# Prompt attention of a two-layer trunk: from head pairs in a loop to single heads in a pipeline, and PSUM banks released one by one

## What is computed

```python
def latent_attention(q_lat, q_pe, rows, q_pos, k_pos):
    c_kv, k_pe = rows[:, :KV_LORA], rows[:, KV_LORA:]
    s = (jnp.einsum('qhr,kr->hqk', q_lat, c_kv, preferred_element_type=jnp.float32)
         + jnp.einsum('qhp,kp->hqk', q_pe, k_pe, preferred_element_type=jnp.float32)) * SOFTMAX_SCALE
    s = jnp.where(k_pos[None, None, :] <= q_pos[None, :, None], s, NEG_INF)
    p = jax.nn.softmax(s, axis=-1)
...
        hp = layer_norm(ALPHA * hp + mix_p, ln_g[i, 0], ln_b[i, 0])
        hp = layer_norm(ALPHA * hp + swiglu(hp, ffn_w_gate[i], ffn_w_up[i], ffn_w_down[i]), ln_g[i, 1], ln_b[i, 1])
```

## Time and profile before

| | us |
|---|---|
| median of three executions | 2686.84 (2685.57 to 2687.7) |
| the profiled execution, its own time | 2684.7 |
| span of its instructions | 2682.9 |
| PE busy with matmuls | 2553.1 (95% of the span) |
| DVE / ACT / POOL busy | 1005.3 / 567.6 / 585.6 |
| mean granted TensorE clock | 0.974 of full speed |

### The profile page before, as it was taken

The page is one execution under the profiler, slowest core; times in us unless marked ns, Lnnn a source line. Parts: engine busy times, 40 slices in busy tenths (PEclk is TensorE's granted clock), DMA queues, the critical chain, the costliest instruction groups (busy, mean ns, idle before and its releaser), DMA issues.

```text
span 2682.9 us, 34788 instructions
## 1 busy us (share of the span) xinstructions
PE 2553.1 (95%) x13203; PEld 2122.1 (79%) x13203; DVE 1005.3 (37%) x1489; ACT 567.6 (21%) x948; POOL 585.6 (22%) x290
## 2 busy tenths in 40 slices
PE   8899999999999889899999999988999999999996
PEld 7789888898889776585857584447889988899885
DVE  3433333333333642333333333422333333333336
ACT  2411011110111342332323232433111111111112
POOL 2422222222222410000000000232222222222225
PEclk9999999999999989999999999988999999999998
DMA  5201110111101111000000002232101111011111
GB/s 165 55 24 47 47 47 23 47 47 47 47 23 47 44 48 43 16 1 31 0 19 12 16 0 75 80 122 55 46 25 47 47 47 40 30 47 47 47 31 67
DMA packets 130114, 117.37 MB, mean 44 GB/s; under 512 B 8704, under 2 KB 117208, under 8 KB 130048
## 3 DMA queue, kind: packets, MB, share of 16 engines
q1 hardware_dynamic: 130064, 116.70, 14.6%
HBM read 110.81 MB, written 6.42 MB: 44 GB/s over the span
## 4 chain that ended last, share of the span: by engine, by line
PE 92%; DVE 4%; issue 2%; ACT 1%; POOL 0%; DMA 0%; SPq 0%; ACTq 0%; DVEq 0%
PE ps L557 22%; PE ps L558 21%; PE ps L559 21%; PE ps L922 4%; PE ps L911 4%; PE ps L806 2%; PE ps L895 2%; PE ps L978 1%; PE ps L780 1%; PE ps L822 1%; PE ps L811 1%; PE ps L627 1%; PE ps L953 1%; PE ps L851 1%; PE ps L937 1%
## 5 line engine op out<-in xcount | busy, mean ns | idle before, releaser
L557 PE MATMUL ps<-XH,WGH 128*128 128x368 f32 x2112 | 699.8, 331 | 17.6 <-POOL WGL L1700 13.5
L558 PE MATMUL ps<-XL,WGH 128*128 128x368 f32 x2112 | 700.0, 331 | 0.0
L559 PE MATMUL ps<-XH,WGL 128*128 128x368 f32 x2112 | 697.2, 330 | 0.0
L1452 DVE TENSOR_TENSOR XR<-XR,ps 128x1024 f32<-128x1024 f32 x378 | 461.5, 1221 | 105.7 <-PE ps L559 105.7
L557 PEld LDWEIGHTS ps<-XH,WGH 128*128 128x128 f32 x2112 | 398.5, 189 | 22.3 <-issue 18.9
L1437 DVE TENSOR_TENSOR HF<-SG,ps 128x368 f32<-128x368 f32 x132 | 71.0, 538 | 917.8 <-PE ps L559 912.6
L558 PEld LDWEIGHTS ps<-XL,WGH 128*128 128x128 f32 x2112 | 398.0, 188 | 1.8
L559 PEld LDWEIGHTS ps<-XH,WGL 128*128 128x128 f32 x2112 | 398.2, 189 | 0.0
L557 PE MATMUL ps<-WDH,HH 128*128 128x512 f32 (+1 forms) x792 | 329.4, 416 | 9.6 <-DVE XR L1452 9.6
L1691 POOL TENSOR_TENSOR HL<-HF,HH 128x368 fp32r<-128x368 f32 x132 | 129.8, 983 | 853.0 <-DVE HH L1441 853.0
L559 PE MATMUL ps<-WDH,HL 128*128 128x512 f32 (+1 forms) x792 | 314.9, 398 | 0.0
(11 more groups left out here) (205 smaller groups left out, 2725.8 us busy)
## 6 DMA issues: line engine op xcount, KB each, us to landing
RAWG<-ffn_w_gate SPq DMA_DIRECT2D x44, 512.0 KB, 4.7
RAWG<-ffn_w_up SPq DMA_DIRECT2D x44, 512.0 KB, 5.9
RAWD<-ffn_w_down SPq DMA_DIRECT2D x44, 512.0 KB, 3.7
CR<-cache_mla_l SPq DMA_DIRECT2D x64, 160.0 KB, 2.6
XR<-x_prompt SPq DMA_DIRECT2D x8, 512.0 KB, 12.4
WOP<-mla_w_o SPq DMA_DIRECT2D x4, 1024.0 KB, 5.0
WOA<-mla_w_o SPq DMA_DIRECT2D x1, 4096.0 KB, 17.3
o_y_prompt<-XR SPq DMA_DIRECT2D x8, 512.0 KB, 2.6
```

The source lines that it names most:

```text
L557: pe.matmul(out, w[0], x[0], start=start, stop=False)
L558: pe.matmul(out, w[0], x[1], start=False, stop=False)
L559: return pe.matmul(out, w[1], x[0], start=False, stop=stop)
L1452: dve.tensor_tensor(XR[0:r, t, :], XR[0:r, t, :], bank2(4 + 2 * w, r), ALU.add).then_inc(s_row[2 * l + 1], 1)
```

## The change

- **Attention.** The loop of head pairs becomes one straight list of 72 units, head by head. Between the steps of a unit PE issues "side" pieces from a list (`SIDE`, `PLAN`): the 11 projection pieces of the next head and the 16 output pieces (one matmul of 512 columns each) of the head before, up to three pieces in a unit: one ahead of the transposes, one ahead of the value product, one behind it. Head 0's projections come before all units, the last head's output pieces after them. `SHARE` says how many pieces each unit takes.
- **Banks.** Scores of even units use banks 0 and 1, those of odd units bank 2; a piece that doesn't fit goes to bank 6 (`EXTRA`). Value products and output transposes use bank 3, probability transposes 4 and 5, side pieces 6 and 7 in turn, but 7 alone while bank 6 is held for scores.
- **Values** are projected for one head at a time (128 columns for each weight load instead of 256). An output piece is added to `XR` by DVE on its own (512 columns).
- **Meta unit.** Its scores have 80 rows instead of 16, and transposes and value products always take 128 rows. POOL clears the columns of `PR` behind a unit's keys.
- **SwiGLU.** `down_tile`, `last_down` and `down_add` wait, signal and add by banks of 512 columns instead of pairs.
- The weights of a head are loaded on their own, two heads ahead. `c_band_meta` has 80 rows.

```diff
+BANKS = 4
+SHARE = ([(1, 1, 0)] * 5 + [(0, 1, 0)] + [(0, 0, 0)] * 3, [(1, 1, 1)] * 9, [(0, 0, 0)] + [(0, 1, 1)] * 8)
...
+        EXTRA = 6
+        ORDER = ((7, 8, 6, 0, 5, 1, 4, 2, 3), (0, 7, 8, 6, 3, 5, 1, 4, 2))
+        UNITS = [(h, q) for h in range(H) for q in ORDER[h % 2]]
...
+                for x_, n_ in enumerate(parts):
+                    PLAN[-1].append(range(len(SIDE), len(SIDE) + n_))
+                    SIDE += own[:n_]
+                    own = own[n_:]
+                    later = range(u_, u_ + 2) if x_ == 0 else range(u_ + 1, u_ + 3)
+                    held = any(extra(e) for e in later if e < NU)
+                    for f_ in range(n_):
+                        BANK.append(13 - EXTRA if held else 13 - BANK[-1] if BANK[-1] in (6, 7) else 6)
...
 # PE, down_tile
-                pe.wait_ge(s_row[2 * l + 1], NT * n + t + 1)
                 for half in (0, 1):
                     ds = slice(half * 512, half * 512 + 512)
-                    ins = split_product(ps[0:r, 4 + 2 * w + half, :], (HH[:, b, cols(t)], HL[:, b, cols(t)]),
-                                        (WDH[:, ds], WDL[:, ds]), True, True)
-                ins.then_inc(f_dmm[l], 1)
+                    pe.wait_ge(s_row[2 * l + 1], 2 * NT * n + 2 * t + half + 1)
+                    split_product(ps[0:r, 4 + 2 * w + half, :], (HH[:, b, cols(t)], HL[:, b, cols(t)]),
+                                  (WDH[:, ds], WDL[:, ds]), True, True).then_inc(f_dmm[l], 1)
...
 # PE, attention
+            def side(f):
+                kind, h, k = SIDE[f]
+                s, b = h % 2, BANK[f]
+                before = [x for x in range(f) if BANK[x] == b]
+                if before:
+                    wait_side(pe, before[-1])
...
+            for u in range(NU):
+                groups = chunks(UNITS[u][1])
+                for f in PLAN[u][0]:
+                    side(f)
+                pe.wait_ge(h_ex, ex_count(u))
+                pe.wait_ge(h_z, u + 1)
+                for x, g in enumerate(groups):
+                    if x == 2:
+                        followers(u)
+                    probability_group(u, x, g)
+                if len(groups) < 3:
+                    followers(u)
+                for f in PLAN[u][1]:
+                    side(f)
+                values(u)
+                for f in PLAN[u][2]:
+                    side(f)
...
 # ACT, attention
+            for u in range(NU):
+                h = UNITS[u][0]
+                for f in PLAN[u][0]:
+                    side_act(f)
+                if u >= 1:
+                    output_rows(u - 1)
+                if u + 1 < NU:
+                    exponentials(u + 1)
+                for x, g in enumerate(chunks(UNITS[u][1])):
+                    k = GROUP_AT[u] + x
+                    if k % 2 == 0:
+                        evacuate_probabilities(act, copy, u, k, g).then_inc(h_ta, 1)
+                for part in PLAN[u][1:]:
+                    for f in part:
+                        side_act(f)
+                if u % NQ == 2 and h + 1 < H:
+                    rope_queries(h + 1)
...
 # DVE, down_add
-                dve.tensor_tensor(XR[0:r, t, :], XR[0:r, t, :], bank2(4 + 2 * w, r), ALU.add
-                                  ).then_inc(s_row[2 * l + 1], 1)
+                for half in (0, 1):
+                    ds = slice(half * 512, half * 512 + 512)
+                    dve.wait_ge(f_dmm[l], 1 + 2 * NT * n + 2 * t + half + 1)
+                    dve.wait_ge(s_row[2 * l + 1], 2 * NT * n + 2 * t + half + 1)
+                    dve.tensor_tensor(XR[0:r, t, ds], XR[0:r, t, ds], ps[0:r, 4 + 2 * w + half, :], ALU.add
+                                      ).then_inc(s_row[2 * l + 1], 1)
...
 # POOL, attention
+            for u in range(NU):
+                n = unit_q(UNITS[u][1])[2]
+                if u >= 2:
+                    pool.wait_ge(h_t, GROUP_AT[u - 1])
+                pool.memset(PR[:, u % 2, n:(n + P - 1) // P * P], 0.0).then_inc(h_z, 1)
```

More of the change, by code:

```diff
@@ L290, in pieces @@
[L290 to L315, removed]
+        KSPLIT = (0, 352, 704, KEYS)
+        def projection(h):
+            return ([("q", h, k) for k in range(3)] + [("k", h, k) for k in range(3)] + [("t", h, 0)]
+                    + [("v", h, k) for k in range(3)] + [("l", h, 0)])
+        def output(h):
+            return [("o", h, k) for k in range(2 * (NT - 1))]
@@ new lines, in hybrid_trunk @@
+        SIDE = projection(0)
+        BANK = [f % 4 for f in range(len(SIDE))]
+        PLAN = []
+        for h_ in range(H):
+            own = (projection(h_ + 1) if h_ + 1 < H else []) + (output(h_ - 1) if h_ > 0 else [])
+            share = SHARE[0 if h_ == 0 else 2 if h_ == H - 1 else 1]
+            assert sum(sum(x) for x in share) == len(own) and len(share) == NQ
+            for parts in share:
+                PLAN.append([])
+                u_ = len(PLAN) - 1
+                for x_, n_ in enumerate(parts):
[6 more added lines that the diff above has]
+                        BANK.append(13 - EXTRA if held else 13 - BANK[-1] if BANK[-1] in (6, 7) else 6)
@@ new lines, in wait_side, with wait_projection, evacuate_side @@
+        def wait_side(eng, f):
+            if f in SIDE_DVE:
+                eng.wait_ge(h_fd, dve_sides(f))
+            else:
+                eng.wait_ge(h_fa, act_sides(f))
+        def wait_projection(eng, h):
+            last = SIDE.index(("l", h, 0))
+            eng.wait_ge(h_fa, act_sides(last))
+            eng.wait_ge(h_fd, dve_sides(last))
+        def evacuate_side(eng, copy, f, low):
+            kind, h, k = SIDE[f]
+            s = h % 2
+            b = BANK[f]
+            src = ps[:, b, :]
+            eng.wait_ge(h_fill, f + 1)
@@ new lines, in scores @@
+            def scores(u):
+                h, q = UNITS[u]
+                if u % NQ == 0:
+                    wait_projection(pe, h)
+                    pe.wait_ge(h_ql, h + 1)
+                if extra(u) and u >= 2:
+                    before = [f for f in range(PLAN[u - 2][1].start) if BANK[f] == EXTRA]
+                    if before:
+                        wait_side(pe, before[-1])
+                for bank, lo, hi in pieces(u):
+                    ins = score_piece(u, bank, lo, hi)
+                ins.then_inc(h_s, 1)
@@ new lines, in values @@
+            def values(u):
+                h, q = UNITS[u]
+                ta, td = groups_done(u)
+                pe.wait_ge(h_ta, ta)
+                if td:
+                    pe.wait_ge(h_td, td)
+                if u >= 1:
+                    pe.wait_ge(h_te, u)
+                last = (unit_q(q)[2] - 1) // P
+                for c in range(last + 1):
+                    ins = pe.matmul(ps[:, 3, 0:VH], PTS[:, u % 2, c, :], VT[:, c, h % 2, :],
+                                    start=(c == 0), stop=(c == last))
+                ins.then_inc(h_pv, 1)
@@ new lines, in _ @@
+            for f in range(len(projection(0))):
+                side(f)
+            pe.wait_ge(h_kr, 2)
+            pe.wait_ge(h_init, 3)
+            scores(0)
+            scores(1)
+            for u in range(NU):
[6 more added lines that the diff above has]
+                    if x == 2:
+                        followers(u)
+                    probability_group(u, x, g)
[5 more added lines that the diff above has]
+                for f in PLAN[u][2]:
+                    side(f)
@@ L929, in page_unit @@
+            out_transpose(NU - 1)
+            for f in LAST_SIDE:
+                side(f)
+            pe.wait_ge(h_fa, len(SIDE_ACT))
+            pe.wait_ge(h_fd, len(SIDE_DVE))
             def page_unit(s, k, b):
```

585 lines of the change are left out of this document (287 added, 298 removed).

## The result

| | before | after | ratio, 95% interval |
|---|---|---|---|
| first comparison, median of 4 runs each | 2686.20 us | 2614.94 us | 0.9742 (0.9720 to 0.9764) |
| the changed kernel again, in a later comparison (7 and 4 runs) | 2683.88 us | 2624.12 us | 0.9776 (0.9760 to 0.9792) |

Forecast: 2651 us, range 2612 to 2679. The change gained 71 us in the first comparison and 60 in the second, where 36 were forecast. So the question is where 24 to 35 us came from that no term of the sum held.

The account below looks back on a forecast made before the run. PE, busy 95% of the span, was taken as the bound. Terms -30 + 2 - 62 + 4 + 50 = -36 against 2684.7 us gave 2649, or 2651 us at the median; range 2612 to 2679 us.

Parts of the forecast that it names:

- Banks in the down pass: SwiGLU down passes: PE's wait for DVE's add goes when banks are freed singly, 40 x 0.75 = -30 us.
- Last down passes: Down passes at each layer's end, where DVE is the bound: two adds replace one, +2 us (0 to +4).
- Stalls that go: Prompt attention: all present PE stalls vanish except the very first queries' 1.8 us, -62 us.
- Change no number of columns that matter; nothing, between -1 and +1: Attention: more rows in meta scores, transposes and value products cost PE nothing, between -1 and +1 us.
- +4 us to the value pieces: Attention value projections by single heads: 36 matmuls of 128 columns at 0.246 us, 8.86 for 7.88 us, four times.
- New waits: Attention pipeline: PE waits for ORW (16 + 15 us), shared banks (18) and list ends (1), sum +50 us.
- full cover: Rival: the attention pipeline covers nearly all, new waits 10 to 25 us instead of 50; 2619 us, chance 0.27.
- Clock, slower than before: Rival: many 1 to 2 us waits in each attention head keep lowering the clock; 2695 us, chance 0.08.
- DVE bounds the pass: Rival: half adds cost DVE 0.72 us or more, so down passes gain only -10; 2671 us, chance 0.10.
- The attention gives nothing at all: Rival: attention waits of 58 us and more, only down passes gain; 2659 us, within the forecast's own range.
- What was to show it: Profile signs: 12.5 us down passes without the wait, attention about 545 us, ORW and bank 7 waits, projection-only stage only for head 0.

Follow-up runs that it names:

- experiment 2: Changed kernel with the meta band (its load and matmuls) cut back to 16 rows: 2631.45 us, ratio 0.9779.
- experiment 6: Kernel before with down passes by single banks, the 80-row band and last value chunks on 128 partitions, but no pipeline: 2617.53 us, ratio 0.9756.
- experiment 1: Kernel before with only the down-pass edits of the change (banks given back singly, adds of 512 columns): 2648.95 us, ratio 0.9859.
- experiments 7 to 9: Changed kernel with ORW copied at its own step's end (2606.90 us), then also rotary work on POOL (2593.73 us), then also side pieces redistributed (2586.89 us).

## Why the forecast was right in sign and 24 to 35 us short

1. *Banks in the down pass, -30*: right. 40 x (13.24 - 12.50) = -30 us, and the two stages together gave -31 to -33. DVE's adds take 0.69 us and are no bound, so that rival fell.
2. *Last down passes, +2*: not seen; nothing in the stages of the SwiGLUs is left for it (-31 to -33 in all, where -28 was forecast).
3. *Stalls that go, -62*: a little too large. Before, PE idled 553.2 - 518.1 = 35 us in the attention and spent 34 us at half clock, worth 17 at most: 52 us. After: 45 us idle, 7 to 14 us at half clock, 48 to 52 us. Both sums leave out some 8 us, by my estimate: the views show such a matmul 0.275 us long where they start 0.112 apart, so idle time is some 0.16 us short at each wait, of which there are 48 before and 52 after. With it the stalls before come to 60 us, and the new waits to 53.
4. ***"Change no number of columns that matter; nothing, between -1 and +1"*: this is the step that failed.** The 80-row band is worth -7 to -8 us (experiment 2) and the full last chunk -24 to -27 us (experiment 6); of the product I had counted columns only, of the band I had written nothing, and left out that a matmul on 16 rows costs more than one on 128 when its neighbours have 128. The row I had in hand says it: the eight value products of the earlier trace rows end with the short one, and 1.97 us over eight gave me "0.246 each", where seven stand at 0.224 and the last takes the rest, 0.40. With that mean I then charged +4 us to the value pieces; they take 36 x 0.111 = 4.0 us a head, 8.0 for a pair against 7.88, so +0.5 for the four pairs.
5. *New waits, +50*: right as a sum (44.9 us of idle time) and in kind, in part by luck in the sizes. For `ORW` PE waited 19.6 us (forecast 16 + 15): 12.6 behind the rotary copies, 2.7 us three times, 1.0 three times and 1.4 once (forecast 2.3 seven times), and 7 behind projection pieces. At shared banks and low parts it was 16 us (forecast 18). Another 9 us of waits of other kinds, for `VT`, `PR`, `QPS` and `OT` above all, stood in no line of the forecast and made up most of the difference.

So in the attention the pipeline's old stalls and new waits cancel, and experiment 6 shows just that: +2 to +5 us. Add -24 in the value products, -8 at the start, -31 to -33 in the SwiGLU stages and -2 in the latents (most of it there with the edit of experiment 1 alone, its cause not tried): -60 to -65 us, against -60.6 between the profile of before and that of the later comparison. In the first comparison the sample attention, at a higher clock, adds 8 to 9.

The result lies in the stated range by luck: the range was drawn down to 2612 us to take in full cover, and full cover did not happen.

*The rivals.* "Full cover" had said 2619 us, the number nearest to the result, and its mechanism did not happen: PE still waited 45 us. It came only with experiments 7 to 9, and then the kernel stood at 2587. "Clock, slower than before" fell: the clock in the attention went up (0.97 to 0.99) with 10 us more of idle time. "DVE bounds the pass" fell with 12.47 us. "The attention gives nothing at all" is what the pipeline did, but not the whole change.

*What was to show it.* Right: the pass of 12.5 us, the adds of 0.69, the wait of the weight load gone, `ORW` behind the rotary copies once a head (though 1.0 to 2.7 us), the waits at shared banks. Wrong: the attention at 545 us; it took 531 to 534.

Still open: why the clock in the sample attention takes one of two courses with the same work, between comparisons and within one.

## What to carry to other kernels

Count changes of tile size as well as columns: a matmul on 16 or 64 partitions between matmuls on 128 cost 0.34 to 0.38 us here for the round trip, the same for either, so pad it with zeros if it stands alone and put short ones side by side if there are more. When a rewrite wins, run the old structure with the rewrite's small edits: here they held all of the gain outside the down passes, and the pipeline none until its own last waits were taken away. And a mean over a group of like instructions hides the one that is not like the others; look at single starts before using it as a price.

## What the runs showed of the hardware

- Start-to-start distances of records of 128-column matmuls at the full clock: 112 ns on 80 or 128 partitions; 205, 213, 200 to 202 and 213 ns around one chunk on 16 or on 64 (0.38 us more than four times 112); 112 ns again from one short chunk to the next. At the lower clock the round trip in the band cost 0.58 us (0.72 for 0.43, twice).
- The same 664 matmuls of the sample attention took 162.2 us at a mean clock of 0.97 and 170.3 at 0.92, in two profiles of one kernel.
- More short chunks went with more time at the lower clock in the attention: 7 and 14 us with none (two profiles), 24 with one in a product, 34 with two, though two side by side are no more changes of size than one. What causes it was not tried.
- The three profiles with 16-row matmuls in the band came to the full clock at 23.8 to 25.5 us, the ten with 80 rows at 13.2 to 16.2, by the clock's record and the distances between matmuls.
- POOL copied 64x1104 elements from SBUF to SBUF in 1.10 us, as fast as ScalarE (1.12), and VectorE beside it kept its times.
